# Gate matmuls of the recurrent branch: one F32 pass or three F32R passes over split operands

## The chip, the cores and the metric

The kernel runs on one core of one Trainium2 chip. The metric is the device time of one execution in microseconds (us); lower is better.

## What is computed

One layer of a block with three parts: a mixer, a merge of its branches, and a feed-forward part with a convolution. All arrays are float32. There are 1024 tokens and 256 context tokens, of width 1024. The change lies in the mixer, whose recurrent branch takes its input through a short convolution and then computes two gates for each of two directions:

```python
def rglru_coeffs(xc, wa, ba, wx, bx, lam):
    xb = xc.reshape(b_, t_, LRU_BLOCKS, LRU_BLOCK_W)           # 8 blocks of 128 channels
    r = sigmoid(einsum('btnk,nkj->btnj', xb, wa) + ba)
    i = sigmoid(einsum('btnk,nkj->btnj', xb, wx) + bx)
    log_a = -LRU_C * r * softplus(-lam)
    a = exp(log_a)
    b = sqrt(-expm1(2.0 * log_a)) * i * xc
    return a, b                                                # h[t] = a[t] * h[t-1] + b[t]
...
xr = dwconv(xr, lru_conv_w, lru_conv_b, LRU_CONV_LEFT)         # 4 taps
cr = dwconv(cr, lru_conv_w, lru_conv_b, LRU_CONV_LEFT)
h_x, h_c = rglru_bidirectional(xr, cr, ...)
y_rnn_x = h_x * gelu(gx)
```

Beside it the mixer computes a neighbourhood attention of 16 heads, with normalized and rotated queries and keys and a bias by relative position.

## The kernel before

**Turns.** The mixer runs eight turns, one for each block of 128 channels and, at the same time, for a pair of attention heads. Each engine has its own program `turn(i, first, last)`, and the order of the work on each engine is the order in which these programs issue it. Turn 0 and turn 7 have orders of their own; the six turns between them are the same.

**High and low parts.** Most matmuls take both operands in two parts: a high part, cast to F32R by ScalarE (`split_hi`), and a low part, the difference of the value and its high part, subtracted by VectorE (`split_low`, L1311). Three passes (high by high, low by high, high by low) go into the same bank: `three_passes` (L45 to L47) for the query tiles, `chunk` (L857 to L859) for the projections `fm`. The gates do not: `gate_pieces` (L890) issues one F32 matmul of the convolution's output `xc` with the weights `lw`. One such matmul stands in the trace as two records of TensorE.

**One middle turn, on TensorE.** The projection of the gelu gate (`fm` of `G`, two halves), with the last group of the previous turn's attention between them; ten query tiles `q_tile`, the first two with 256 columns and the others with 384; behind tiles 0, 1, 2 the gate pieces of direction 0, two at a time, and behind tiles 4, 5, 6 those of direction 1 (`GATES_AFTER`). There are six pieces a direction: pieces 0 to 2 give `r`, pieces 3 to 5 give `i`, over the context (256 columns) and two halves of the tokens (512 each, `SEGS`). A piece waits until the bank that it writes is free (`f_free`), which means until ScalarE has evacuated the piece two before it. Then come the projection of the next turn's recurrent input (`XR`), transposes, the first scores, the projections `MR` and `MN`, and the attention: for each of 16 units `prob_transposes` (L948, L953), `scores` (L930 to L935), and `weighted_values` (L968, L986).

**On the other engines in that turn.** ScalarE splits the query weights, evacuates `gel`, the tiles (`q_evac`, L1096 and L1101) and the gate pieces (L1091), then computes the decays (`decays`, L1114 to L1118) and the root (`root`, L1122), and splits the weights of `XR` and `MR` behind the fifth tile. VectorE subtracts the low parts of the query weights, runs the convolution (`conv`, L1341 and L1344), the sums of the last attention group of the turn before (`outputs`, L1500 and L1503), then `head_squares` for every tile, `gated_input` (L1359), `complement` (L1363), `scan` (L1370, L1374), `mean_squares` (L1392), the low parts of `XR` and `MR`, and from `inverse_roots` (L1400 to L1402) on the normalizations and rotations of keys and queries (L1407 to L1427), which the transposes wait for. GpSimd raises the mean squares to a power (`inverse_root`, L808), adds masks to the bias (L816, L819, L823) once the bias has landed and the convolution is done, finishes the sigmoids of the output gates (L798, L801), and copies low parts of keys (`exchange_low`, L790). SP issues the loads: the gate weights `lw` at the start of a turn, and the weights of each unit once `w_lo` says that its slot of `raw` has been split.

**Slots.** `fh` and `fl` hold the high and low parts of projection weights in two slots. Slot 0 holds `XR` and then `MN`. `ORDER` gives the place of each unit in the counts `w_hi` and `w_lo`; loads and matmuls wait for these counts through `split_count`.

## Time and profile before

| | us |
|---|---|
| median of 3 runs | 2171.84 |
| lowest and highest | 2170.0 and 2172.96 |
| the profiled execution | 2171.01 |
| span of its core | 2169.2 |
| granted TensorE clock over the span | 0.99 of full |
| TensorE (PE) busy | 2086.3, 96% |
| VectorE (DVE) busy | 1569.0, 72% |
| ScalarE (ACT) busy | 1053.6, 49% |
| GpSimd (POOL) busy | 346.0, 16% |

The span is the stretch of the profiled execution in which the engines work; the little that is left lies around it. The mixer covers the span up to about 1220 us, and one middle turn takes 140.5 us. Busy shares are means over stages with different limits: what a change inside a turn is worth is read from the queues of the engines in that turn, at the moments where one waits for another. In a timeline, times are counted from the start of the span.

### The profile page before, as it was taken

What the parts mean: (1) busy time and instruction counts of PE and PEld (TensorE: products, weight loads), DVE (VectorE), ACT (ScalarE), POOL (GpSimd) and SP (SyncE); (2) the same over time, 40 slices, a digit from 0 to 9 for tenths busy, and PEclk for the clock granted to TensorE, in tenths of its full rate; (3) what the DMA queues carried; (4) which work ended last, traced back from release to release, by engine and by line L of the source; (5) the groups of instructions that cost most, each with busy time, mean ns of one, the idle gap of its engine ahead of it and who ended that gap; (6) DMA issues with size and microseconds to landing.
All of it is one profiled execution on the core that took longest, in us unless ns stands there. A gap on an engine that the chain in (4) does not pass through costs nothing.

```text
span 2169.2 us, 28185 instructions
## 1 busy us (share of the span) xinstructions
PE 2086.3 (96%) x10750; PEld 1769.4 (82%) x10750; DVE 1569.0 (72%) x2758; ACT 1053.6 (49%) x1614; POOL 346.0 (16%) x234
## 2 busy tenths in 40 slices
PE   5999999999999999999997999998999999999999
PEld 1788888988889889888886788886888888888887
DVE  6688598685985968859759766667998888863433
ACT  3466665765766656766576410003444334433221
POOL 0031221221312221122122000000111111110000
PEclk9999999999999999999999999998999999999999
DMA  8421212012112120121202574452222221146552
GB/s 322 109 63 40 70 41 81 11 57 64 35 43 64 52 69 30 40 71 40 71 1 98 184 274 157 148 197 70 78 78 88 87 77 69 68 161 207 185 183 89
DMA packets 85654, 209.91 MB, mean 97 GB/s; under 512 B 24592, under 2 KB 30096, under 8 KB 85392
## 3 DMA queue, kind: packets, MB, share of 16 engines
q1 hardware_dynamic: 63360, 182.95, 24.8%
q0 software_dynamic: 5760, 20.97, 2.8%
q10 hardware_dynamic: 16400, 4.19, 0.9%
q8 instruction: 85, 1.39, 0.3%
q14 instruction: 49, 0.40, 0.1%
HBM read 171.39 MB, written 40.89 MB: 98 GB/s over the span
## 4 chain that ended last, share of the span: by engine, by line
PE 79%; DVE 11%; ACT 4%; issue 1%; DMA 0%; POOL 0%; SPq 0%; ACTq 0%; DVEq 0%; POOLq 0%
PE banks L47 14%; PE banks L45 14%; PE banks L46 14%; PE banks L986 4%; PE banks L2108 4%; PE banks L2106 4%; PE banks L2107 4%; PE banks L857 4%; PE banks L859 4%; PE banks L858 4%; PE banks L890 3%; DVE probT_low L1486 2%; PE banks L948 2%; DVE prob L1478 1%; PE banks L930 1%
## 5 line engine op out<-in xcount | busy, mean ns | idle before, releaser
L45 PE MATMUL banks<-qh,xnh 128*128 128x384 f32 (+1 forms) x640 | 223.1, 349 | 0.3 <-PEq L211 0.3
L857 PE MATMUL banks<-xnh,wh 128*128 128x512 f32 (+1 forms) x536 | 211.7, 395 | 4.0 <-ACT stage L1091 3.6
L47 PE MATMUL banks<-qh,xnl 128*128 128x384 f32 (+1 forms) x640 | 207.4, 324 | 0.0
L46 PE MATMUL banks<-ql,xnh 128*128 128x384 f32 (+1 forms) x640 | 207.3, 324 | 0.0
L859 PE MATMUL banks<-xnh,wl 128*128 128x512 f32 (+1 forms) x536 | 204.8, 382 | 0.0
L858 PE MATMUL banks<-xnl,wh 128*128 128x512 f32 (+1 forms) x536 | 204.4, 381 | 0.0
L1486 DVE TENSOR_TENSOR probT_low<-banks,probT_high 128x512 fp32r<-128x512 f32 (+2 forms) x256 | 138.8, 583 | 56.2 <-ACT probT_high L1159 55.1
L46 PE MATMUL banks<-yl,wh 128*128 128x512 f32 x404 | 157.3, 389 | 0.0
L47 PE MATMUL banks<-yh,wl 128*128 128x512 f32 x404 | 157.2, 389 | 0.0
L45 PE MATMUL banks<-yh,wh 128*128 128x512 f32 x404 | 157.2, 389 | 0.0
L1159 ACT CAST probT_high<-banks 128x512 fp32r<-128x512 f32 (+2 forms) x256 | 117.1, 510 | 59.9 <-PE banks L948 51.0
L1354 DVE TENSOR_REDUCE ssq<-sqs 128x4 f32<-128x256 f32 (+1 forms) x80 | 31.0, 389 | 143.5 <-ACT sqs L1101 143.2
L2021 POOL TENSOR_TENSOR conv_d<-conv_d 128x1024 f32<-128x1024 f32 x22 | 69.7, 3169 | 382.9 <-ACT conv_d L2147 307.3
L1149 ACT ACTIVATE prob<-prob,stat 128x768 f32<-128x768 f32 (+1 forms) x128 | 128.2, 1002 | 1.4 <-DVE stat L1481 1.2
L45 PEld LDWEIGHTS banks<-qh,xnh 128*128 128x128 f32 x640 | 120.7, 189 | 9.0 <-issue 8.1
L46 PEld LDWEIGHTS banks<-ql,xnh 128*128 128x128 f32 x640 | 120.7, 189 | 8.3 <-issue 7.7
L47 PEld LDWEIGHTS banks<-qh,xnl 128*128 128x128 f32 x640 | 120.6, 188 | 0.0
L859 PEld LDWEIGHTS banks<-xnh,wl 128*128 128x128 f32 x536 | 101.5, 189 | 19.9
L857 PEld LDWEIGHTS banks<-xnh,wh 128*128 128x128 f32 x536 | 102.0, 190 | 18.2 <-issue 3.8
L2401 DVE TENSOR_TENSOR yl<-sw_d,yh 128x512 fp32r<-128x512 f32 x44 | 30.4, 691 | 118.6 <-ACT yh L2223 118.6
L1736 ACT CAST wh<-raw 128x1024 fp32r<-128x1024 f32 x22 | 23.2, 1055 | 189.1 <-PE banks L47 159.3
L986 PE MATMUL banks<-probT_high,vS 128*128 128x256 f32 x448 | 114.0, 293 | 0.0
(346 smaller groups left out, 5764.6 us busy)
## 6 DMA issues: line engine op xcount, KB each, us to landing
raw<-w_ff SPq DMA_DIRECT2D x33, 512.0 KB, 3.7
raw<-w_down SPq DMA_DIRECT2D x33, 512.0 KB, 4.5
raw<-w_fm SPq DMA_DIRECT2D x32, 512.0 KB, 6.5
raw<-w_qkv SPq DMA_DIRECT2D x24, 512.0 KB, 3.9
raw<-w_mix SPq DMA_DIRECT2D x24, 512.0 KB, 4.9
h_d<-conv_d SPq DMA_DIRECT2D x22, 512.0 KB, 2.6
sw_d<-h_d SPq DMA_DIRECT2D x44, 256.0 KB, 3.1
raw<-w_modT SPq DMA_DIRECT2D x16, 512.0 KB, 4.5
```

Source lines behind the costliest of these rows:

```text
L45: pe.matmul(out, w_hi(k), x_hi(k), start=(k == 0), stop=False)
L46: pe.matmul(out, w_hi(k), x_lo(k), start=False, stop=False)
L47: last = pe.matmul(out, w_lo(k), x_hi(k), start=False, stop=(k == chunks - 1))
L857: pe.matmul(out, fh[:, s, k, :], xnh[:, k, c0:c1], start=(k == 0), stop=False)
L858: pe.matmul(out, fh[:, s, k, :], xnl[:, k, c0:c1], start=False, stop=False)
L859: return pe.matmul(out, fl[:, s, k, :], xnh[:, k, c0:c1], start=False, stop=(k == KC - 1))
L986: last = pe.matmul(dst, vS[:, s, h, :], moving, start=(n == 0 and part == 0), stop=(n == len(blocks) - 1 and part == 1))
L1149: act.activation(p, p, ACT.Exp, bias=stat[:, u, 1:2], scale=-1.0, accum_out=stat[:, u, 2:3]).then_inc(exp_done, 1)
L1159: act.copy(probT_blocks(pth, u, bank), probT_bank(u, bank)).then_inc(pt_hi, 1)
L1486: dve.tensor_tensor(probT_blocks(ptl, u, bank), probT_bank(u, bank), probT_blocks(pth, u, bank).bitcast(F32), ALU.subtract).then_inc(pt_lo, 1)
L2106: pe.matmul(out, w_hi_c[:, m, :], h_slot(xh, c), start=(k == 0), stop=False)
L2107: pe.matmul(out, w_hi_c[:, m, :], h_slot(xl, c), start=False, stop=False)
```

## The change

Each gate matmul becomes three F32R passes, high weights by high input, high weights by low input, low weights by high input. For that the gate weights and the convolution's output are split in every turn: ScalarE casts the weights (`gate_weights_high`) and the three segments of `xc` (`gate_input_high`), VectorE subtracts the four low parts (`gate_weights_low`, `gate_input_low`) right behind the convolution, the last of them behind the sums of the previous turn's last attention group. The parts lie in slot 0 of `fh` and `fl` and in memory that `stage` and `pad` and their neighbours use at other times. `XR` needs slot 0 too, so its split moves behind the gates: on ScalarE behind the last gate pieces' evacuation, on VectorE behind the first rotation, and `MR` is split before it. In the middle turns `gated_input` of direction 0 goes ahead of the fourth `head_squares`. The convolution signals its context part and its token part apart, and what waited for the whole waits for the second signal. On TensorE the waits for the landed weights and for the convolution are gone; the first three pieces wait for the low parts instead.

```diff
+        lwh, lwl = fl[:, 0, 0:4, :], fl[:, 0, 4:8, :]
+        xcl_tokens = fh[:, 0, :, :].rearrange("p k c -> p (k c)")
...
-        ORDER = {Q0: 0, Q1: 1, Q2: 2, XR: 3, MR: 4, MN: 5, G: 6}
+        ORDER = {Q0: 0, Q1: 1, Q2: 2, MR: 3, XR: 4, MN: 5, G: 6}
...
-                pool.wait_ge(conv_done, i + 1)
+                pool.wait_ge(conv_done, 2 * i + 2)
...
-                if d == 0 and pieces[0] == 0:
-                    pe.wait_ge(lw_in, i * 16 + 16)
-                    pe.wait_ge(conv_done, i + 1)
                 for n in pieces:
                     c0, c1 = SEGS[n % 3]
                     j = gate_use(i, d, n)
                     pe.wait_ge(f_free, f_count(i, j) - 2)
-                    pe.matmul(f_bank(j)[:, 0:c1 - c0], lw[:, 2 * (n // 3) + d, :], xc[:, c0:c1],
-                              start=True, stop=True).then_inc(f_full, 1)
+                    if d == 0 and n < 3:
+                        pe.wait_ge(gate_lo, 4 * i + n + 2)
+                    m = 2 * (n // 3) + d
+                    out = f_bank(j)[:, 0:c1 - c0]
+                    pe.matmul(out, lwh[:, m, :], xch_of(n % 3), start=True, stop=False)
+                    pe.matmul(out, lwh[:, m, :], xcl_of(n % 3), start=False, stop=False)
+                    pe.matmul(out, lwl[:, m, :], xch_of(n % 3), start=False, stop=True).then_inc(f_full, 1)
...
+            def gate_weights_high(i):
+                act.wait_ge(lw_in, i * 16 + 16)
+                act.copy(lwh, lw[:, :, :]).then_inc(gate_hi, 1)
+
+            def gate_input_high(i, seg):
+                c0, c1 = SEGS[seg]
+                act.wait_ge(conv_done, 2 * i + (1 if seg == 0 else 2))
+                act.copy(xch_of(seg), xc[:, c0:c1]).then_inc(gate_hi, 1)
...
                 gelu(i, 0)
+                gate_weights_high(i)
+                gate_input_high(i, 0)
                 if not last:
                     gelu(i, 1)
+                gate_input_high(i, 1)
+                gate_input_high(i, 2)
...
-                if not last:
-                    split_hi(XR, raw_count(XR, i))
                 split_hi(MR, raw_count(MR, i))
                 q_evac(i, 6)
                 gate_pieces(i, *(GATES_FIRST if first else GATES_AFTER)[6])
                 if first:
                     q_evac(i, 7)
                     gate_pieces(i, *GATES_FIRST[7])
+                if not last:
+                    split_hi(XR, raw_count(XR, i))
...
+            def gate_weights_low(i):
+                dve.wait_ge(gate_hi, 4 * i + 1)
+                dve.tensor_tensor(lwl, lw[:, :, :], lwh.bitcast(F32), ALU.subtract).then_inc(gate_lo, 1)
+
+            def gate_input_low(i, seg, first):
+                c0, c1 = SEGS[seg]
+                dve.wait_ge(conv_done, 2 * i + 2)
+                dve.wait_ge(gate_hi, 4 * i + seg + 2)
+                if seg == 0 and not first:
+                    dve.wait_ge(stage_out, i * 64)
+                dve.tensor_tensor(xcl_of(seg), xc[:, c0:c1], xch_of(seg).bitcast(F32), ALU.subtract).then_inc(gate_lo, 1)
...
                 conv(i, first)
+                gate_weights_low(i)
+                gate_input_low(i, 0, first)
+                gate_input_low(i, 1, first)
                 if not first:
                     outputs(i - 1, GROUPS_ATT - 1, False)
-                for s in range(4):
+                gate_input_low(i, 2, first)
+                early = not first and not last
+                for s in range(3):
                     head_squares(i, s)
+                if early:
+                    gated_input(i, 0)
+                head_squares(i, 3)
...
-                if not last:
-                    split_low(XR, i)
                 split_low(MR, i, last)
...
                 rotate(1, 0, krot[0])
+                if not last:
+                    split_low(XR, i)
```

## Rows read from the trace of the kernel before

**Rows 1.** The page, busy time, share of the span and instructions.
```profile
PE 2086.3 (96%) x10750; PEld 1769.4 (82%) x10750; DVE 1569.0 (72%) x2758; ACT 1053.6 (49%) x1614; POOL 346.0 (16%) x234
```
**Rows 2.** Timeline, TensorE, middle turn: start us, duration us, instruction, [idle before <- releaser].
```profile
376.14 0.28 PE L45 MATMUL banks<-qh,xnh 128*128 128x256 f32 x1
...
379.02 1.45 PE L890 MATMUL banks<-xc,lw 128*128 128x256 f32 x4
...
383.17 1.45 PE L890 MATMUL banks<-xc,lw 128*128 128x512 f32 x4
...
388.62 1.88 PE L890 MATMUL banks<-xc,lw 128*128 128x512 f32 x4
...
398.67 1.45 PE L890 MATMUL banks<-xc,lw 128*128 128x256 f32 x4
...
404.12 1.50 PE L890 MATMUL banks<-xc,lw 128*128 128x512 f32 x4
...
455.59 0.63 PE L948 MATMUL banks<-cst,prob 128*128 128x128 f32 x4 [1.27 <-DVE probT_low L1486]
```
**Rows 3.** Timeline, VectorE, the same turn.
```profile
411.46 0.18 DVE L1400 TENSOR_TENSOR rstd<-rstd 128x24 f32<-128x24 f32 x1 [0.41 <-POOL rstd L808]
...
418.07 0.42 DVE L1354 TENSOR_REDUCE ssq<-sqs 128x4 f32<-128x256 f32 x1 [0.22 <-ACT sqs L1101]
...
445.62 0.16 DVE L1481 TENSOR_TENSOR stat<-stat 128x1 f32<-128x1 f32 x1
...
446.21 0.15 DVE L1563 TENSOR_SCALAR stat<-one 128x1 f32<-128x1 f32 x1 [0.43 <-PE banks L935]
```
**Rows 4.** Timeline, ScalarE, the same turn.
```profile
376.35 0.60 ACT L1091 ACTIVATE gel<-banks 128x512 f32<-128x512 f32 x1 [3.18 <-PE banks L859]
...
403.53 1.05 ACT L1091 ACTIVATE gR<-banks,lp 128x256 f32<-128x256 f32 x2
...
446.07 0.93 ACT L1149 ACTIVATE prob<-prob,stat 128x768 f32<-128x768 f32 x1
```
**Rows 5.** Timeline, VectorE and GpSimd, before this turn and in turn 0.
```profile
365.49 1.23 DVE L1311 TENSOR_TENSOR ql<-raw,qh 128x1024 fp32r<-128x1024 f32 x1
...
366.63 2.06 DVE L1311 TENSOR_TENSOR ql<-raw,qh 128x1024 fp32r<-128x1024 f32 x1
...
365.71 1.90 POOL L801 TENSOR_TENSOR stage<-stage,half_one 128x512 f32<-128x512 f32 x1
...
123.05 1.76 DVE L1311 TENSOR_TENSOR wl<-raw,wh 128x1024 fp32r<-128x1024 f32 x1
...
121.94 1.79 POOL L816 TENSOR_TENSOR bias<-bias,cst 128x256 f32<-128x256 f32 x1 [1.06 <-DMA bias<-bias_d]
...
123.69 3.07 POOL L819 TENSOR_TENSOR bias<-bias,cst 128x896 f32<-128x896 f32 x1
```
**Rows 6.** Timeline, VectorE and GpSimd, behind the convolution.
```profile
376.71 0.43 DVE L1500 TENSOR_TENSOR bot<-banks,bot 64x256 f32<-64x256 f32 x1
...
376.83 0.74 POOL L816 TENSOR_TENSOR bias<-bias,cst 128x256 f32<-128x256 f32 x1 [9.22 <-DVE xc L1344]
...
377.52 2.12 POOL L819 TENSOR_TENSOR bias<-bias,cst 128x896 f32<-128x896 f32 x1
...
379.71 4.03 POOL L823 TENSOR_TENSOR bias<-bias,cst 128x1792 f32<-128x1792 f32 x1
```
**Rows 7.** Timeline, VectorE and GpSimd, at the mean squares' power.
```profile
407.26 4.16 POOL L808 TENSOR_TENSOR rstd<-rstd,power 128x24 f32<-128x24 f32 x1 [23.52 <-DVE rstd L1392]
...
407.31 1.26 DVE L1311 TENSOR_TENSOR wl<-raw,wh 128x1024 fp32r<-128x1024 f32 x1 [0.19 <-ACT wh L1085]
```
**Rows 8.** Timeline, TensorE, in turn 0 and in the last turn.
```profile
95.67 1.56 PE L890 MATMUL banks<-xc,lw 128*128 128x256 f32 x4 [0.16 <-DMA lw<-lru_w]
...
142.27 1.12 PE L910 MATMUL banks<-cst,qkv 128*128 128x128 f32 x4 [3.49 <-DVE qrotA L1427]
...
1079.27 1.10 PE L890 MATMUL banks<-xc,lw 128*128 128x256 f32 x3 [0.21 <-issue]
```

More of the change, by code:

```diff
@@ L508, in mixer_programs @@
         ptl = sbuf(st, "probT_low", [P, RING * 7, P], F32R)
+        with ExitStack() as gate_parts:
+            xcl_context = sbuf(gate_parts, "xcl_context", [P, C], F32R)
         stage = sbuf(st, "stage", [P, HALF])
@@ L522, in mixer_programs @@
         yT = sbuf(st, "yT", [P, 2, 256])
+        with ExitStack() as gate_parts:
+            xch = sbuf(gate_parts, "xch", [P, 1288], F32R)
         pad = sbuf(st, "pad", [P, 1288])
@@ L528, in mixer_programs @@
         sinT = cst[:, P + 3 * GW + NT * HD:].rearrange("p (t f) -> p t f", f=HD)
+        lwh, lwl = fl[:, 0, 0:4, :], fl[:, 0, 4:8, :]
+        xcl_tokens = fh[:, 0, :, :].rearrange("p k c -> p (k c)")
+        xch_of = lambda seg: xch[:, (2, 5, 5)[seg] + SEGS[seg][0]:(2, 5, 5)[seg] + SEGS[seg][1]]
+        xcl_of = lambda seg: xcl_context[:, :] if seg == 0 else xcl_tokens[:, SEGS[seg][0] - C:SEGS[seg][1] - C]
         S, lower, F_ps = banks
@@ L541, in mixer_programs @@
         lw_in = sem("b_lw_in")
+        gate_hi, gate_lo = sem("b_gate_hi"), sem("b_gate_lo")
         decayed = sem("b_decayed")
@@ L1198, in turn @@
                         split_hi(u, raw_count(u, i))
+                if not first:
                     bottoms(i - 1, GROUPS_ATT - 1)
@@ L1244, in turn @@
                     gate_pieces(i, *GATES_FIRST[7])
+                if not last:
+                    split_hi(XR, raw_count(XR, i))
+                if first:
                     decays(i, 1)
@@ L1348, in conv @@
                             then(last)
-                last.then_inc(conv_done, 1)
+                    last.then_inc(conv_done, 1)
+            def gate_weights_low(i):
[8 more added lines that the diff above has]
+                dve.tensor_tensor(xcl_of(seg), xc[:, c0:c1], xch_of(seg).bitcast(F32), ALU.subtract).then_inc(gate_lo, 1)
             def head_squares(i, s):
@@ L1520, in turn @@
                     head_squares(i, 4)
-                gated_input(i, 0)
+                if not early:
+                    gated_input(i, 0)
                 complement(i, 0)
```

## The prediction, made before the changed kernel ran

> **What bounds the kernel now.** I read the page first, then the queue of TensorE in one middle turn of the mixer, then the queues of VectorE, GpSimd and ScalarE at the same moments. TensorE is busy for 96% of the span [rows 1], so any step it gets shorter by could count. The mixer runs eight turns. The six middle ones repeat with a period of 140.5 us, so I follow the one whose first query tile starts at 376.14 and multiply by six. In it TensorE goes from tile to gate to tile without a gap, and stops once for long: at 455.59 it has stood 1.27 us for VectorE's low half of the first transposed probabilities [rows 2]. So the turn has two limits in series: TensorE up to about the last query tile, and from there VectorE, which between 411.46 and that wait idles only 0.22 and 0.43 us in the rows shown, for ScalarE and for scores [rows 3]. A gain on TensorE before that wait only makes the wait longer, unless VectorE's own chain starts earlier too.
>
> **The gate matmuls.** Tile 0 takes 379.02 - 376.14 = 2.88 us for 24 passes of 256 columns, 0.12 each. From 379.02 to 383.17 lie two gate pieces (256 and 512 columns) and tile 1, so the pieces take 4.15 - 2.88 = 1.27 us. From 383.17 to 388.62 the same pair and tile 2 of 24 passes of 384 columns: 5.45 - 1.28 = 4.17 us, 0.174 a pass. From 388.62 to 398.67 two 512-column pieces and two tiles: 10.05 - 8.34 = 1.71 us [rows 2]. A pass therefore costs some 0.45 ns a column, and F32 gates 1.67 ns a column. Three F32R passes cost 0.36 us for 256 columns and 0.68 for 512: the pair falls from 1.28 to 1.04, the double 512 from 1.71 to 1.36. A turn has four pairs and two doubles, 4 x 0.24 + 2 x 0.35 = 1.65 us, over eight turns 13 us at most. That the three passes might not be cheaper is excluded by these rows.
>
> One piece of it is not paid out. At 404.12 TensorE reaches the third piece of direction 1, which needs the bank that ScalarE empties from 403.53 on, some 0.45 us of work [rows 4]. That chain hangs on tile 4, not on the gates, so what the pair at 398.67 saves is lost again in a wait.
>
> **The new splits.** ScalarE gets four casts (weights, three input pieces). A 512-column evacuation takes 0.60 us and stands at 376.35 [rows 4]; with two more behind it the last cast is done by about 378.0, ahead of tile 0's evacuation at 379.2. ScalarE idles there, so I charge nothing. If the cover were gone, tile 0's evacuation would be late by the 1.8 us of the casts, and tile 3 is the first to want it.
>
> VectorE gets four subtractions right behind the convolution, which ends at 376.7. One of 1024 columns takes 1.23 us, 1.14 from start to start (365.49 to 366.63) [rows 5]; I estimate 0.65 for 512 and 0.4 for 256. Alone they would be done for piece 1 at 378.5, before TensorE asks at 379.4. But they do not stand alone. The same convolution count releases GpSimd's three bias additions: 0.74 us at 376.83, 2.12 at 377.52, 4.03 at 379.71 [rows 6]. In the kernel before, what VectorE does beside them is a sum with one operand in PSUM, 0.43 us, untouched [rows 6]. The new subtractions have both operands in SBUF, and such instructions and GpSimd's exclude each other in this trace. The weight split at 366.63 takes 2.06 us instead of 1.23 while GpSimd's multiplication from 365.71 takes 1.90. In turn 0 the split at 123.05 takes 1.76 beside a bias addition of 1.79 instead of 0.74; and the next addition, 3.07 instead of 2.12, has waited for that split [rows 5]. They also take turns: where both wait, the one that did not run last goes next. The split at 123.05 ended at 124.81, so it went between two additions that GpSimd issues back to back.
>
> With that the order after the convolution is: weights low to 377.4; addition 1 to 378.1; context low to 378.5; addition 2 (2.1) to 380.6; first token half low to 381.2; then the old sums of the last attention group, free of the conflict, to 382.1, while addition 3 (4.0) runs to 385.2; second token half low to 385.9. TensorE asks for the first half at 379.4 and gets it at 381.3, ends the pair at 382.0 and tile 1 at 384.9; asks for the second half and gets it at 386.0; ends the pair at 387.0, tile 2 at 391.2, the double at 392.6, where it was at 390.3. It enters tile 3 about **2.2 us late** instead of 0.24 + 0.24 + 0.35 = 0.8 early. The removed waits for the weights' load and the convolution cost nothing in this turn. Behind the waiting gates on TensorE stand the query tiles, and behind those everything else. The last group's sums come 4.5 us later; tile 2 and the store of that group wait for them and have over 2 us left. The context part also waits for the last store of the stage; GpSimd wrote it by 367.6 [rows 5], which leaves the store over 9 us.
>
> The shared port is the subject of the Trainium skill, SBUF — State Buffer, section "Who interferes with whom": a VectorE instruction with two SBUF inputs contends with a GpSimd instruction that reads SBUF, and the loser blocks for the whole instruction. The additions agree with that, 2.06 for 1.23. The power of the mean squares does not: it runs 4.16 us from 407.26, and a split of two SBUF inputs takes 1.26 beside it at 407.31 [rows 7]. By the Trainium skill both splits would have stood until 411.4 and taking one away from there would shorten the chain by 1.1 us a turn, 7 us in all; by the row it shortens nothing, since the power, not the splits, is what ends last there. I go by the row.
>
> **The rnn weights moved.** VectorE's split of them, 1.14 us, leaves a place where VectorE then waits 0.41 for the power anyway (411.46), and goes behind the rotation, into a stretch without idle time but the 0.22 at 418.07 [rows 3]. The load of G that SP holds for this split comes later by about 12 us and is first read in the attention, over 40 us on. ScalarE's cast (about 1 us) delays the decays and tile 7's evacuation, not past tile 8's. TensorE needs the split after tile 9 and has it some 4 us earlier. Cost on VectorE's chain: 1.14 - 0.22, about 0.9. The earlier multiplication of the gated input removes nothing from the path, because ScalarE's root waits for tile 4. POOL's bound on the bias count is the same moment as before.
>
> **One middle turn.** VectorE's chain starts from the root behind tile 4, so 2.2 late; plus 0.9 makes 3.1; the 0.43 us of idle time at 446.21 gives back up to that, 2.7; but the exponential at 446.07 [rows 4], which ScalarE began 0.3 us behind its input of 445.62 + 0.16 [rows 3], then comes 2.8 late, and with it the transposed queries behind it. TensorE, by then only 1.4 late, waits for it. I take 2.75, times six: **16.5**.
>
> **First and last turn.** In turn 0 the gates wait for the weights' load until 95.67 [rows 8]. ScalarE now waits for it with the first cast, and a cast, a half's cast and a subtraction follow before the second piece can start: about 98.3 where it was 96.1, 2.1 us late. The additions come only at 121.9 there. The wait of 3.49 us at 142.27 [rows 8] shows VectorE as the limit, and its chain gets 1.14 for the moved split and up to 0.8 from a changed order with the additions: between 1.0 and 2.1, I take 1.9. In the last turn TensorE reaches the gates at 1079.27, right when the convolution ends [rows 8], so the whole queue shows: the second piece starts at about 1083.8 where it was 1079.8, 4.0 late, of which some 1.0 comes back through shorter pieces: 3.0.
>
> **The sum.** 16.5 + 1.9 + 3.0 = 21.4. The profiled execution took 2171.01 us around a span of 2169.2, and would take 2192.4; it is 0.8 below the median of 2171.84, so the forecast is **2193**.
>
> **Rivals.** (1) *VectorE wins every time, or the new subtractions do not conflict*: the gates are met as computed without GpSimd. It decides at 379.4: the first half must be split by then. TensorE enters tile 3 0.8 early, VectorE's chain gains 0.8, loses 0.9, gains up to 0.4: 0 to 0.3 a turn, -1; turn 0 +1.5, last +1: 2173, no change. For it speaks only that VectorE issues first; the 2.06 at 366.63 speaks against. Chance 0.14. (2) *The full TensorE gain arrives*, 1.45 a turn, 2160. It needs slack on VectorE that [rows 3] do not show: 0.04. (3) *GpSimd keeps the port between additions 1 and 2*, or the later sigmoids of GpSimd collide with the late VectorE. The first moves the second piece to 385.3, 2.9 more a turn, 2211; the second costs one instruction of about 1.0 a turn, 2200. The row at 123.05 speaks against the first. Together 0.12. (4) *Only the long third addition is met*, the others slip past: about 1 us a turn, 2178 to 2186, 0.06.
>
> **How the numbers follow.** The forecast's own range, 2187 to 2199, has 0.64. Unknown sizes (0.65 and 0.4 for the subtractions, the releases of about 0.1) move it by some 0.5 a turn. The range 2175 to 2205 takes in (4), part of (1) and most of (3) and leaves out about 0.2. A difference of 0.2%, 4.3 us, is about what a measurement of this kernel can tell from none. Faster has (2) and an edge of (1): 0.05; same the rest of (1): 0.12; slower 0.83.
>
> **What would show it.** Right: the subtractions of the token halves at 2 to 4 us instead of 0.65 beside GpSimd's additions; TensorE idle about 1.9 and 1.1 us before the second and third gate piece; a middle turn of 143.2 us; the idle time before 455.59 grown to about 2.6. Wrong: subtractions of 0.65 beside 4.0 us additions (rival 1), or a turn under 140.5.

## The result and the profile after

The changed kernel takes 2207.24 us (median of 5 runs, 2204.89 to 2212.96) against 2171.84: a ratio of 1.0171, 95% interval 1.016 to 1.0183. It is 35.4 us slower, where the forecast was 21 and the range ended at 2205. The profiled execution took 2207.24 us around a span of 2205.4. The first section of its page (engine, busy time and share of the span, instructions) stands against [rows 1]:

```profile
PE 2084.5 (95%) x10846; PEld 1785.6 (81%) x10846; DVE 1627.7 (74%) x2790; ACT 1066.3 (48%) x1646; POOL 353.1 (16%) x234
```

TensorE is busy for 1.8 us less, VectorE for 58.7 us more, and the span is 36.2 us longer. The convolution's first instruction on VectorE cuts the mixer into turns. The start moved by -1.3 us (over all profiles of the study it lies between 86.2 and 88.3 us), turn 0 grew by 4.6, five middle turns by 4.0 each and one by 8.5, and what lies behind the last convolution's start by 4.2.

A middle turn splits at five instructions of VectorE's queue, which every kernel of this study has. In the kernel before, for the turn at 370.02, they are the convolution (L1341), the mean squares (L1392), their roots (L1400), the first small operation behind the scores (L1481) and the second pair of `qpS` subtractions (L1445). The table gives the time from each to the next, as the difference of two starts in the timeline of VectorE. It is the same within 0.1 us in all middle turns but at most one, of which below; f13 has a second one, 0.2 us longer. The runs of the next section stand in it too.

| kernel | conv. to mean square | to roots | to small op. | to `qpS` | to next conv. | turn |
|---|---|---|---|---|---|---|
| before | 36.92 | 4.52 | 34.16 | 5.04 | 59.86 | 140.50 |
| **changed** | 38.65 | 5.56 | 34.97 | 5.52 | 59.86 | 144.55 |
| e1, additions later | 36.21 | 5.56 | 34.97 | 5.52 | 59.87 | 142.13 |
| e2, MR split behind squares | 38.63 | 4.92 | 34.96 | 4.80 | 59.87 | 143.20 |
| e3, orders alone | 36.92 | 4.52 | 35.02 | 5.52 | 59.86 | 141.84 |
| e4, cut F32 gates | 36.11 | 5.56 | 33.83 | 5.09 | 59.85 | 140.44 |
| f11, the same, eight copies | 36.13 | 4.52 | 33.84 | 4.80 | 59.87 | 139.15 |
| f13, changed, eight copies | 38.65 | 4.52 | 34.98 | 5.06 | 59.87 | 143.10 |
| f6, e1 and early MR split | 36.22 | 4.52 | 34.98 | 5.07 | 59.87 | 140.66 |
| f9, three repairs, `lw` first | 36.21 | 4.52 | 34.98 | 4.80 | 59.88 | 140.39 |
| f12, XR split early too | 36.24 | 4.52 | 33.85 | 4.82 | 59.87 | 139.29 |

The changed kernel loses 1.73 + 1.04 + 0.81 + 0.48 = 4.06 us a turn, in four places.

**Behind the convolution** (timeline of VectorE, GpSimd and TensorE in one middle turn; start, us, engine, line, operation, operands; in brackets the idle time before and what ended it):

```profile
383.92 0.68 DVE L1380 TENSOR_TENSOR wl<-lw,wl 128x512 fp32r<-128x512 f32 x1
384.52 0.97 DVE L1388 TENSOR_TENSOR xcl_context<-xc,xch 128x256 fp32r<-128x256 f32 x1
385.41 2.59 DVE L1388 TENSOR_TENSOR wh<-xc,xch 128x512 fp32r<-128x512 f32 x1
...
388.95 3.52 DVE L1388 TENSOR_TENSOR wh<-xc,xch 128x512 fp32r<-128x512 f32 x1
...
384.15 1.05 POOL L826 TENSOR_TENSOR bias<-bias,cst 128x256 f32<-128x256 f32 x1 [9.21 <-DVE xc L1371]
385.16 2.29 POOL L829 TENSOR_TENSOR bias<-bias,cst 128x896 f32<-128x896 f32 x1
387.54 4.38 POOL L833 TENSOR_TENSOR bias<-bias,cst 128x1792 f32<-128x1792 f32 x1
...
388.15 0.47 PE L901 MATMUL banks<-xch,wl 128*128 128x512 f32 x1 [1.29 <-DVE wh L1388]
...
392.62 0.47 PE L901 MATMUL banks<-xch,wl 128*128 128x512 f32 x1 [0.67 <-DVE wh L1388]
```

This is the forecast's sequence. The four subtractions and the three additions of [rows 6] alternate. The token halves take 2.59 and 3.52 us for work of 0.68, and TensorE stands 1.29 and 0.67 us before the pieces that want them.

**At the power** (ScalarE's cast of MR, VectorE's mean square, split and roots, GpSimd's power):

```profile
415.08 1.08 ACT L1097 CAST wh<-raw 128x1024 fp32r<-128x1024 f32 x1
...
415.99 0.18 DVE L1431 TENSOR_SCALAR rstd<-ssq 128x24 f32<-128x24 f32 x1
416.26 1.23 DVE L1338 TENSOR_TENSOR wl<-raw,wh 128x1024 fp32r<-128x1024 f32 x1
...
421.55 0.18 DVE L1439 TENSOR_TENSOR rstd<-rstd 128x24 f32<-128x24 f32 x1 [1.69 <-POOL rstd L818]
...
416.31 5.21 POOL L818 TENSOR_TENSOR rstd<-rstd,power 128x24 f32<-128x24 f32 x1 [24.39 <-DVE rstd L1431]
```

In [rows 7] the power started at 407.26 and the split at 407.31, having waited 0.19 us for ScalarE's cast. Here the split starts at 416.26, 0.05 us ahead of the power, and the power takes 5.21 us instead of 4.16. The cast now starts 0.91 us ahead of the mean square, where the kernel before had 0.77, and the split no longer waits for it; e3 and e4 below show what moved it.

**At the scores** (VectorE's small operation, ScalarE's exponential behind it, GpSimd's first sigmoid):

```profile
456.51 0.88 DVE L1520 TENSOR_TENSOR stat<-stat 128x1 f32<-128x1 f32 x1
...
457.42 0.94 ACT L1170 ACTIVATE prob<-prob,stat 128x768 f32<-128x768 f32 x1 [2.71 <-DVE stat L1520]
...
454.85 1.40 POOL L808 TENSOR_TENSOR stage<-stage,one 128x512 f32<-128x512 f32 x1 [9.18 <-ACT stage L1103]
456.32 1.04 POOL L811 TENSOR_TENSOR stage<-stage,half_one 128x512 f32<-128x512 f32 x1
```

and GpSimd's first sigmoid instruction in the kernel before:

```profile
446.31 1.04 POOL L798 TENSOR_TENSOR stage<-stage,one 128x512 f32<-128x512 f32 x1 [11.55 <-ACT stage L1091]
```

There it came 0.69 us behind the small operation, which [rows 3] have at 445.62. The small operation of one column, 0.16 us in [rows 3], takes 0.88: it starts 0.19 us behind a sigmoid instruction and ends with it. 0.24 of the 0.72 us is slack of the exponential, which had waited for ScalarE; 0.48 stays.

**In one turn the weights land late** (ScalarE's cast of `lw`, VectorE's subtractions, TensorE's waits, fifth middle turn):

```profile
817.60 0.62 ACT L1123 CAST wl<-lw 128x512 fp32r<-128x512 f32 x1 [3.47 <-DMA lw<-lru_w]
...
819.00 2.32 DVE L1388 TENSOR_TENSOR xcl_context<-xc,xch 128x256 fp32r<-128x256 f32 x1
821.24 4.45 DVE L1388 TENSOR_TENSOR wh<-xc,xch 128x512 fp32r<-128x512 f32 x1
...
825.84 0.77 PE L901 MATMUL banks<-xch,wl 128*128 128x512 f32 x1 [3.78 <-DVE wh L1388]
```

ScalarE waits for the load 3.47 us instead of the usual 2.2 to 2.5. So little is enough for the two short additions to get the port first, and the first token half then costs 4.45 us instead of 2.59. TensorE stands 1.33 and 3.78 us before its first two gate pieces, 3.15 us more than in the other middle turns; with the clock, of which next, the turn is 4.45 us longer. The same turn is the long one in every profile of the three passes in which the additions start with the convolution's end (148.7 in e2, 150.1 in f1, 148.2 in f13). Why the load is late there was not tried.

**The granted clock falls behind the long waits** (windows of the changed kernel: stretch, its length, busy time of TensorE, its weight loads, VectorE, ScalarE and GpSimd, granted clock, DMA share, GB/s):

```profile
98.20:101.60 3.40, 3.40 (x12) 3.33 (x12) 0.56 (x2) 2.75 (x5) 0.00 (x0) 0.50 1.20 261
825.30:828.70 3.40, 2.86 (x10) 2.60 (x11) 2.13 (x5) 0.69 (x1) 0.00 (x0) 0.50 0.11 39
1115.40:1118.80 3.40, 3.40 (x10) 3.12 (x11) 3.33 (x3) 0.87 (x2) 3.40 (x1) 0.50 0.11 39
```

0.50 of full is the 1.2 GHz level. The three stretches lie in turn 0, in the long turn and in the last turn, each behind TensorE's waits for low parts: 2.24 and 0.46 us, 1.33 and 3.78, 1.72 and 1.91. In the middle turns that wait 1.29 and 0.67 us the clock stays at 1.00, and so it does there in all turns of the kernel before and of e1, where the longest such waits are 1.44 us together in turn 0 and 1.18 in the last. In turn 0, tile 1 takes 5.71 us from its first matmul to the next gate piece, against 4.18 in e1: 1.5 us. What the waits leave unexplained in the long turn and, against e1, in the last one is 1.3 us each. In the long turn of e2, with waits of 1.34 and 3.78 us, the clock is at 0.50 for 6.8 us, and the turn is 5.5 us longer instead of 4.45.

### The profile page after: what moved, and what is told of

It is laid out like the page before. It is cut to its first block, busy times and chain, and to the rows that moved or that the text cites. A ratio compares the mean times of both kernels' runs of the same rounds, so it can differ in the third digit from the quotient of the medians.

```text
span 2205.4 us, 28481 instructions
## 1 busy us (share of the span) xinstructions
PE 2084.5 (95%) x10846; PEld 1785.6 (81%) x10846; DVE 1627.7 (74%) x2790; ACT 1066.3 (48%) x1646; POOL 353.1 (16%) x234
## 4 chain that ended last, share of the span: by engine, by line
PE 60%; DVE 26%; ACT 5%; issue 3%; POOL 2%; DMA 1%; SPq 0%; DVEq 0%; ACTq 0%; POOLq 0%
PE banks L45 12%; PE banks L47 12%; PE banks L46 12%; PE banks L998 4%; PE banks L2154 4%; PE banks L2156 4%; PE banks L2155 4%; DVE probT_low L1525 2%; DVE wh L1388 2%; DVE prob L1517 2%; PE banks L960 1%; POOL rstd L818 1%; DVE xc L1371 1%; DVE wl L1338 1%; DVE swp L1464 1%
## 5 line engine op out<-in xcount | busy, mean ns | idle before, releaser
L45 PE MATMUL banks<-qh,xnh 128*128 128x384 f32 (+1 forms) x640 | 209.4, 327 | 0.3 <-PEq L211 0.3
L818 POOL TENSOR_TENSOR rstd<-rstd,power 128x24 f32<-128x24 f32 (+1 forms) x16 | 65.1, 4071 | 337.1 <-DVE rstd L1431 337.1
```

The source lines that it names most:

```text
L45: pe.matmul(out, w_hi(k), x_hi(k), start=(k == 0), stop=False)
```

## The experiments

Each is given with its median of 4 to 11 runs and the ratio to the kernel before, which had 2170.5 to 2171.0 us on the same chips.

**e1: the bias additions behind the low parts.** It tests the cause of the first place.

```diff
-                pool.wait_ge(conv_done, 2 * i + 2)
+                pool.wait_ge(gate_lo, 4 * i + 4)
```

> The changed kernel with one wait moved: GpSimd's three bias additions start only when all four low parts of the gate operands are stored, instead of with the end of the convolution. Theory (the two engines' two-input operations exclude each other, and each subtraction behind the convolution but the first waits for one bias addition): the token-half subtractions take 0.68 us instead of 2.59 and 3.52, TensorE's waits of 1.29 and 0.67 us before the second and third gate piece go, the one turn of 149.0 us, in which the weights landed late and the three additions got ahead, becomes like the others; a middle turn goes from 144.5 to about 142, the last turn loses some 3 us, the whole is about 20 us faster (near 2187). The power comes later on GpSimd by some 2 us, which costs nothing, since its own mean square is later than that. Rival (ScalarE's casts and the subtractions are late by themselves: the low parts are produced too late whatever GpSimd does): waits and time stay, 2205 to 2209.

Measured: 2184.81 us, 1.0065 (1.0052 to 1.0078), 22.4 below the changed kernel. In the turn at 373.75:

```profile
380.93 0.42 DVE L1388 TENSOR_TENSOR xcl_context<-xc,xch 128x256 fp32r<-128x256 f32 x1
381.56 0.69 DVE L1388 TENSOR_TENSOR wh<-xc,xch 128x512 fp32r<-128x512 f32 x1 [0.22 <-ACT xch L1128]
...
383.20 0.69 DVE L1388 TENSOR_TENSOR wh<-xc,xch 128x512 fp32r<-128x512 f32 x1
...
384.04 0.74 POOL L826 TENSOR_TENSOR bias<-bias,cst 128x256 f32<-128x256 f32 x1 [12.70 <-DVE wh L1388]
...
386.94 4.06 POOL L833 TENSOR_TENSOR bias<-bias,cst 128x1792 f32<-128x1792 f32 x1
```

The subtractions take 0.42 and 0.69 us, both waits of TensorE before gate pieces are gone, the long turn takes 142.45 us, and the rest behind the last convolution's start is 0.3 us longer than before instead of 4.2. The theory holds: the subtractions were late because they and the additions exclude each other. Some 4 of the 22.4 us are the clock, which no longer falls behind the waits (an estimate, the sum of the three costs above). The convolution to the mean square is now 0.71 us *shorter* than in the kernel before: the passes' gain arrives here. Over the whole turn it can be read in TensorE's queue, from the first gate piece to the projection behind the last tile: 43.6 us against 44.8 in the kernel before, so the passes save 1.2 us a turn.

**e2: the MR split behind the power.**

```diff
-                split_low(MR, i, last)
+                if first or last:
+                    split_low(MR, i, last)
                 head_squares(i, 6)
+                if not first and not last:
+                    split_low(MR, i, last)
```

> The changed kernel with the low split of the MR weights put behind the squares of the sixth head pair on VectorE, in the middle turns alone, so that GpSimd's power starts before it. Theory (a power that starts under a running split waits for its end: 5.21 us against 4.16 before the change): the power takes 4.16 again, VectorE's wait for it ends 1.05 us earlier, the whole is about 6 us faster (six turns), unless the small two-input operation behind the scores, which GpSimd's sigmoid blocks for 0.72 us, meets it otherwise. Rival (the power's 5.21 is something else, and the chain behind it is set by TensorE): no change, within 2 us.

Measured: 2200.44 us, 1.0135 (1.0121 to 1.0149), 6.8 below the changed kernel, as expected, but half for another reason. The power takes 4.17 us. The split now ends 0.5 us behind it and holds the roots back, so 0.64 of the 1.04 us comes back there. The other 0.72 comes back at the scores, which VectorE now reaches when the sigmoid does not hold the small operation (4.80).

**e3: the orders alone**, with the F32 gates of before: `ORDER`, the XR split behind the rotation on both engines, `gated_input` ahead of the fourth `head_squares`.

> The kernel before, with its F32 gate matmuls, and only the orders of the change: XR split behind MR, its low part moved behind the second key rotation, the first gated input before the fourth head squares. Theory: the power starts under the running MR split (+1.05 us a middle turn), the XR split now lies on VectorE's chain (+0.9), the softmax has 0.3 of slack: +1.6 a middle turn, with turn 0 and the last some 10 us slower in all (2180 to 2186). If the collision of the small operation behind the scores with the sigmoid appears here too, +0.7 a turn more. Rival (the orders are free, the split was only moved): no change.

Measured: 2181.52 us, 1.0043 (1.0029 to 1.0057), 10.6 us slower. The total was right and half of its reason wrong: the power did not grow. 34.16 became 35.02 for the XR split, and 5.04 became 5.52 for the small operation (0.88 us again). The MR split still waited for ScalarE's cast and started 0.05 us behind the power:

```profile
410.79 1.04 ACT L1085 CAST wh<-raw 128x1024 fp32r<-128x1024 f32 x1
...
411.57 0.18 DVE L1393 TENSOR_SCALAR rstd<-ssq 128x24 f32<-128x24 f32 x1
411.94 1.26 DVE L1312 TENSOR_TENSOR wl<-raw,wh 128x1024 fp32r<-128x1024 f32 x1 [0.19 <-ACT wh L1085]
...
411.89 4.17 POOL L808 TENSOR_TENSOR rstd<-rstd,power 128x24 f32<-128x24 f32 x1 [23.52 <-DVE rstd L1393]
```

**e4: TensorE's gain without splits.** The F32 gate matmuls of before, cut to 216 of 256 and 410 of 512 columns (the last 40 and 102 columns of each gate segment are left out), which saves about what three passes save: 1.4 us a turn in TensorE's queue, against 1.2 in e1.

```diff
-                    pe.matmul(f_bank(j)[:, 0:c1 - c0], lw[:, 2 * (n // 3) + d, :], xc[:, c0:c1],
+                    m = 216 if n % 3 == 0 else 410
+                    pe.matmul(f_bank(j)[:, 0:m], lw[:, 2 * (n // 3) + d, :], xc[:, c0:c0 + m],
```

> The kernel before, its F32 gate matmuls cut to 216 of 256 and 410 of 512 columns, so that TensorE saves about what three F32R passes save (0.24 us a pair, 0.35 a double piece), without splits or casts. The last 40 and 102 columns of each gate segment are left out. Theory (from the head squares on, VectorE's chain sets the turn, and the gate pieces' saving of 1.65 us a turn ends in its idle time of 0.43): 0.3 to 0.8 us a turn, 2167 to 2171. Rival (TensorE's gain arrives whole at the end of the turn): 2158 to 2162.

Measured: 2169.18 us, 0.9991 (0.9983 to 1.0000). The time is that of the theory, its reason is not. The mean square comes 0.81 us earlier and the stretch behind the roots is 0.33 shorter, since VectorE no longer waits for the squares of [rows 3]. Then 1.04 is given back at the power and the small operation takes 0.43 us. The splits start earlier than the power, by 0.04 us:

```profile
406.72 2.03 ACT L1086 CAST wh<-raw 128x1024 fp32r<-128x1024 f32 x2
...
407.63 0.18 DVE L1393 TENSOR_SCALAR rstd<-ssq 128x24 f32<-128x24 f32 x1
407.91 2.39 DVE L1312 TENSOR_TENSOR wl<-raw,wh 128x1024 fp32r<-128x1024 f32 x2
...
407.95 5.21 POOL L808 TENSOR_TENSOR rstd<-rstd,power 128x24 f32<-128x24 f32 x1 [22.71 <-DVE rstd L1393]
```

The same cast and mean square in the kernel before:

```profile
406.17 1.99 ACT L1085 CAST wh<-raw 128x1024 fp32r<-128x1024 f32 x2
...
406.94 0.18 DVE L1392 TENSOR_SCALAR rstd<-ssq 128x24 f32<-128x24 f32 x1
```

e3 and e4 together show what reversed the order of the two starts. The cast starts 0.77 us ahead of the mean square in the kernel before, 0.78 in e3, and 0.91 in e4 and in the changed kernel. e3 exchanges XR and MR and keeps the split's wait; e4 leaves them in their old order and loses it. So it is not the exchange, it is the shorter gate pieces: the cast stands behind their evacuation on ScalarE.

**f1, f5, f8, f11, f13: copies ahead of the splits.** Does the order of two starts decide it, or what stands beside the power? One, four or eight copies of one column on VectorE between the mean square and the splits delay nothing but the splits. f1 (one copy) and f13 (eight) have them in the changed kernel, f5 (one), f8 (four) and f11 (eight) in the kernel of e4, whose gate segments lack their last columns, ahead of both splits.

```diff
+                for c in range(8):
+                    dve.tensor_scalar(stat[:, c, 3:4], one[:, :], 1.0, None, ALU.mult)
                 split_low(MR, i, last)
```

> The changed kernel with one instruction more on VectorE: a copy of one column (128x1, 0.14 us) between the mean square and the low split of the MR weights, in every turn. Theory (it decides alone who is first: with it GpSimd's power starts some 0.1 us ahead of the split instead of 0.05 us behind it, and takes 4.16 us instead of 5.21): a middle turn loses 1.04 us, to about 143.5, or 143.1 where the small operation behind the scores meets the sigmoid less; the whole is 6 to 9 us faster for one instruction more, 2198 to 2201. Rival (the power's length is not decided by the order of the two starts): no change, 2206 to 2208.

> The kernel before with its F32 gate matmuls cut to 216 and 410 columns as before (the last 40 and 102 columns of each gate segment are left out), and with the same one-column copy on VectorE ahead of the two weight splits. Theory (the cut matmuls' gain of 0.82 us up to the mean square was given back there, since the earlier mean square met splits that no longer waited for ScalarE, and the power took 5.21): with the copy the power takes 4.16 again, a middle turn is about 139.4 instead of 140.44, the whole 6 to 7 us faster than without the copy, 2161 to 2164. Rival (TensorE's gain is lost elsewhere): equal to the run without the copy, 2168 to 2170.

Measured: f1 2209.09 us, 1.0176 (1.0162 to 1.0190); f5 2169.45 us, 0.9995 (0.9986 to 1.0003). Neither moved, but neither tells: the copy went into a gap that was there anyway, the split still starts 0.28 us behind the mean square, and the power 0.32 to 0.33.

> The kernel before with the cut F32 gate matmuls (the last 40 and 102 columns of each gate segment are left out) and four one-column copies on VectorE ahead of the weight splits instead of one, since one left the split's start where it was (0.28 us behind the mean square's, the power's is 0.32). Four should put it 0.4 to 0.6 us behind. Theory (who starts first decides): the power takes 4.16 us, mean square to root 4.5 instead of 5.56, a middle turn 139.4 to 139.7 instead of 140.44, the whole 4 to 6 us below 2169. Rival (the power is stretched by whatever stands beside it, in either order): no change, 2168 to 2171.

Measured: 2170.09 us, 0.9997 (0.9988 to 1.0006). The split now starts 0.01 us *behind* the power, and the power still takes 5.25 us, and once 6.39, when it stood behind both splits. The recorded start is not yet the moment from which a split no longer holds the power up.

> The kernel before with the cut F32 gate matmuls (the last 40 and 102 columns of each gate segment are left out) and eight one-column copies on VectorE ahead of the weight splits. Four put the splits' start 0.34 us behind the mean square's, 0.01 us behind the power's, and the power took 5.25 and once 6.39 us. In the kernel before, with 0.05 us between them, it took 4.16. Eight copies should put them some 0.25 us behind the power. Theory (the power takes the port a little after its recorded start and then isn't disturbed by what starts later): power 4.16 to 4.2 us, mean square to root 4.5 us, a middle turn about 139.4 us instead of 140.45, the whole 2162 to 2165. Rival (in the kernel before it was ScalarE's cast, not the order of the starts, that spared the power): power 5.2 again, no change, 2168 to 2171.

Measured: 2160.96 us, 0.9955 (0.9941 to 0.9968). Eight more instructions in every turn make the kernel 8.2 us faster than e4 without them. The splits and the power in f8 (timeline of VectorE, two splits in one line, and of GpSimd):

```profile
407.54 2.38 DVE L1312 TENSOR_TENSOR wl<-raw,wh 128x1024 fp32r<-128x1024 f32 x2
...
407.53 5.25 POOL L808 TENSOR_TENSOR rstd<-rstd,power 128x24 f32<-128x24 f32 x1 [22.71 <-DVE rstd L1393]
```

and in f11:

```profile
405.13 2.35 DVE L1312 TENSOR_TENSOR wl<-raw,wh 128x1024 fp32r<-128x1024 f32 x2
...
404.88 4.17 POOL L808 TENSOR_TENSOR rstd<-rstd,power 128x24 f32<-128x24 f32 x1 [22.71 <-DVE rstd L1393]
```

> The changed kernel with eight one-column copies on VectorE between the mean square and the low split of the MR weights. Theory (the split now starts some 0.25 us behind the power and no longer holds it up): power 4.17 us instead of 5.21, mean square to root 4.52 us, a middle turn 143.1 to 143.5 us instead of 144.55, the whole 6 to 9 us faster, 2198 to 2201. Rival (the order matters only in the kernel before): no change, 2205 to 2209.

Measured: 2200.02 us, 1.0143 (1.0128 to 1.0159), 7.2 below the changed kernel; mean square to roots 4.52 us. So the second place is settled in the changed kernel itself. A split that starts 0.25 us behind the power leaves it at 4.17 us, with as much VectorE work beside it as before.

**f6 and f7: two repairs more.** f6 is e1 with MR split early in the middle turns, in the time that VectorE waits for ScalarE's root (its cast behind the fourth tile). f7 is f6 with the first sigmoid held back.

```diff
                     head_squares(i, 4)
+                if early:
+                    split_low(MR, i, last)
                 scan(i, 0)
...
+                    pool.wait_ge(bound_done, i * ATT + 2)
                     sigmoid(i, F_MR, 0, 4)
```

> The changed kernel with the bias additions behind the low parts (as in the first of these runs), and in the middle turns the MR weights split early, in VectorE's idle time before ScalarE's root (its cast behind the fourth tile on ScalarE), so that no split stands beside the power. Theory: conv start to mean square 36.2 us, power and its wait 4.5, the XR split still on the chain (35.0 to the scores), 4.8 to 5.5 around the softmax, 59.9 behind: 140.4 to 141.1 a middle turn; the whole 6 to 10 us below the run with the additions alone, 2175 to 2179. Rival (the idle time is none: the split delays the root's product): 0 to 1.2 us a turn come back, 2180 to 2188.

> The same, and in all turns but the last GpSimd's first sigmoid waits until the minima of the second scores are stored, so that it meets neither of the small operations behind the scores. Theory: the small operation takes 0.16 us in every middle turn, 140.4 us a middle turn, and in turn 0, where that sigmoid stretched a rotation product from 0.89 to 2.57 us, some 1.5 us go: 2173 to 2176, level with the kernel before or 1 us above it. Rival (a later sigmoid delays TensorE's banks or the stores and costs as much): equal to the run without it or above.

Measured: f6 2175.61 us, 1.0026 (1.0015 to 1.0037); f7 2171.16 us, 1.0007 (0.9998 to 1.0016). Both as expected. In f6 the small operation takes 0.42 us, in f7 0.16; the middle turns of f7 take 140.4 us. The operation in f6:

```profile
452.57 0.42 DVE L1522 TENSOR_TENSOR stat<-stat 128x1 f32<-128x1 f32 x1
```

and in f7, with the sigmoid that now waits for the next one:

```profile
448.92 0.16 DVE L1523 TENSOR_TENSOR stat<-stat 128x1 f32<-128x1 f32 x1
...
450.37 2.22 POOL L808 TENSOR_TENSOR stage<-stage,one 128x512 f32<-128x512 f32 x1 [12.29 <-DVE stat L1523]
```

In the two profiles turn 0 differs by 2.2 us, more than the middle turns' 0.27 explain together. There a sigmoid of the changed kernel had stretched a rotation product from 0.89 to 2.57 us (timeline of VectorE, changed kernel):

```profile
163.67 2.57 DVE L1464 TENSOR_TENSOR swp<-qkv,cst 128x128 f32<-128x128 f32 x4
```

**f9 and f10: the gate weights first.** In turn 0 `lw` is loaded behind 672 KB of constants. f9 is f7 with the two exchanged, f10 the kernel before with the same.

```diff
+            load_gate_weights(0)
             sp.dma_start(cst[:, :], consts).then_inc(const_in, 16)
```

> The changed kernel with the three repairs (bias additions behind the low parts, MR split early, first sigmoid behind the second scores' minima) and, in turn 0, the gate weights loaded ahead of the constants (672 KB) instead of behind them. Theory (TensorE's wait of 3.6 us for the low parts in turn 0 is the late load, which now goes through ScalarE and VectorE before it reaches TensorE): turn 0 loses some 3 us, to about 143 us; the whole is 2167 to 2169, below both kernels. Rival (the constants, now later, are needed as early): no change or slower, 2171 to 2174.

> The kernel before with the same exchange of the two loads in turn 0 alone. TensorE waits there for the gate weights for 0.16 us in the profile shown. Theory: 0 to 2 us faster, 2169 to 2171, less spread between runs. It is the control for the run above: what of that run's gain belongs to the load and not to the repaired gate passes.

Measured: f9 2168.56 us, 0.9993 (0.9984 to 1.0002); f10 2170.19 us, 0.9996 (0.9987 to 1.0005). The exchange gives the repaired kernel 2.6 us and the kernel before 0.9, which is within its interval. With all that the change is level with the kernel before, no more: the 1.14 us of the XR split (33.84 to 34.98) eat the passes' gain.

**f12: the gate parts elsewhere.** XR could not be split before the last gate because the parts lie in its slot. f12 is f9 with them in memory that is idle in the middle turns, and splits XR there before the fourth tile's squares; the gate weights are then cast and subtracted in two halves, and ScalarE casts XR behind the second tile.

```diff
+        qkv_tail = qkv_r[:, 7:10, :].rearrange("p t c -> p (t c)")[:, 0:1024]
...
+            return (qkv_tail if moved(i) else xcl_tokens)[:, SEGS[seg][0] - C:SEGS[seg][1] - C]
...
+            return (qkv_r[:, 0:2, 0:P], lwh_tail[:, :, :]) if moved(i) else (lwh[:, 0:2, :], lwh[:, 2:4, :])
...
+            return lw_r[:, :, :] if moved(i) else lwl
...
                 if early:
                     gated_input(i, 0)
+                    split_low(XR, i)
```

> The repaired kernel (bias additions behind the low parts, MR split early, first sigmoid behind the second scores, gate weights first in turn 0), and in the middle turns the gate parts in memory that is idle then (the tail of the query and key tiles, the gate weights' own place, the upper half of the sigmoid's stage), so that the XR split needn't wait for the gate passes and stands in VectorE's idle time between the third and the fourth tile. Theory (the XR split's 1.15 us on the chain is all that is left): 36.2 + 4.5 + 33.8 + 4.8 + 59.9 = 139.2 us a middle turn instead of 140.4, the whole 7 us below 2168.6, 2161 to 2163. Rival (the early splits, the copy in two halves and the earlier loads meet other work): 2165 to 2170.

Measured: **2161.48 us**, 0.9958 (0.9946 to 0.9971) against the kernel before and 45.8 us below the changed one, 139.3 us a middle turn. It beats both. The XR split in VectorE's idle time, and the wait for the power's end with no split beside it:

```profile
387.99 1.22 DVE L1373 TENSOR_TENSOR wl<-raw,wh 128x1024 fp32r<-128x1024 f32 x1
...
402.17 0.18 DVE L1474 TENSOR_SCALAR rstd<-ssq 128x24 f32<-128x24 f32 x1
...
406.69 0.18 DVE L1482 TENSOR_TENSOR rstd<-rstd 128x24 f32<-128x24 f32 x1 [0.67 <-POOL rstd L842]
...
402.49 4.17 POOL L842 TENSOR_TENSOR rstd<-rstd,power 128x24 f32<-128x24 f32 x1 [19.23 <-DVE rstd L1474]
```

## Why the prediction was right and wrong

Its direction and its main mechanism held, its size did not: 14 us too little.

- *The gate passes* (0.24 a pair, 0.35 a double, 1.65 a turn, 0.24 of it lost in a wait): right in kind, a little too high. In e1 the pairs save 0.24, 0.20, 0.06 and 0.17 and the doubles 0.27 each, 1.2 us where I had 1.4; the 0.06 is the pair that I had written off. e4, which saves 1.4, moves the mean square by 0.81, and f11 shows 1.35 at the end of the turn.
- *TensorE enters tile 3 2.2 us late*: the sequence held to the instruction; the mean square came 1.73 late. The subtractions took 0.68 and 0.42 us for my 0.65 and 0.4. e1 shows the cause.
- *The XR split moved*, 0.9: 0.81 here, 0.86 in e3.
- *The power*, of which I wrote that taking a split away "shortens nothing": right for an absent split (4.17 us in f6), and the step that failed all the same. From [rows 7] I read that the power doesn't mind a split. The row shows that it doesn't mind one that starts 0.05 us after it. I did not ask what had let the power go first: the split's 0.19 us wait for ScalarE's cast. The shorter gate pieces take that wait away (e4), since the cast follows their evacuation and starts 0.13 us earlier against the mean square; I had followed their gain on TensorE alone. Missing: 1.04 a turn, 6 us in all. The Trainium skill, SBUF — State Buffer, "Who interferes with whom", has the loser block for the whole instruction. By that rule a power that starts second waits for the split, and here it does, 1.05 and once 2.23 us. By the same rule a split that starts second would wait for the power, and here it does not, 1.26 us in [rows 7]. My verdict "by the row" set the rule aside for both orders when the row spoke of one.
- *The exponential's slack of 0.3*: 0.24. But the operation ahead of it was late itself, by 0.72. I had priced such a meeting with the sigmoids at 1.0 a turn and left it to a rival of 0.12 shared chance, although VectorE would come 3 us later into a stretch where GpSimd is active. [rows 3] gave the operation's time, 445.62, and the same trace has the sigmoid at 446.31. It is a second failed step: 0.48 a turn net, 3 us.
- *The removed waits cost nothing; ScalarE's casts are free*: true in five turns of six. The wait for the load had not gone, it had moved to ScalarE, ahead of the additions' race for the port: 4.45 us in one turn, of which 3.15 are waits and the rest goes with the clock at 0.50.
- *First and last turn*, 1.9 and 3.0: they grew by 4.6 and 4.2. I had put nothing for the clock, and it took 1.5 and 1.3 us. In the last turn that is the 1.2 that was missing, and e1, with a wait of 1.18 us instead of 3.63 and the clock at 1.00, gives back 3.9. In turn 0 the first gate piece came 2.1 us later, as forecast; the sigmoids' 1.68 was missing beside the clock. f7 gets 2.2 us back there against f6, and f9 5.5 against f7, in their profiles. The load varies between profiles: ScalarE waits for it 7.7 us in f7, 6.3 in the changed kernel and 5.1 in e1, and in f7 the clock falls behind it as well.
- *The sum*: 6 x 2.75 = 16.5 stands against 28.7 for the middle turns. Over six turns the power was short by 6.2 us, the end of the chain by 5.0 (0.35 a turn was to come back, 0.48 was lost), the late load and the clock behind it by 4.5; the first place and the XR split were 3.3 too high.
- *Rival 2*, the full gain of 1.45 a turn, I gave 0.04 because [rows 3] show no slack on VectorE. That was the wrong test. Those rows begin with the roots; what lies before them, tiles, squares and root, is set by TensorE, and gets earlier with it. f11 and f12 show 1.35 and 1.2 us of it.

## What to carry to other kernels

When two engines share a port, read from the trace who starts first and by how much, and what holds the other back: a margin of 0.05 us decided 1.05 us a turn here, and 0.13 us gained in a third engine's queue reversed it. New two-input work on VectorE belongs where GpSimd is quiet, or GpSimd's long work is made to wait for it: one moved wait returned 22 of 35 us. And before a gain is written off against a later limit, see what sets that limit's start; a gain of 1.4 us a turn looked lost in e4 (0.06) and was there (1.35) as soon as a collision behind it was removed.

## What the runs showed of the hardware

- The power of 24 columns runs 4.16 us and lets two-input splits run beside it at full speed, but waits for one that is under way. Being 0.01 us ahead in the records is not enough (5.25 us), 0.05 is (4.16).
- An operation of one column, 0.16 us, takes 0.88 us beside a GpSimd instruction of 512 columns in every middle turn of the changed kernel, and 1.00 in the last turn of f6. Each time it ends with that instruction.
- Behind the convolution the granted clock fell to 0.50 (1.2 GHz) for 3.4 us after TensorE had stood for 2.24 and 0.46, 1.33 and 3.78, and 1.72 and 1.91 us, and stayed at 1.00 after 1.29 and 0.67. It cost 1.3 to 1.5 us each time.
- A one-column copy behind a small VectorE instruction costs nothing when a dependent one follows: the split's start moved by less than 0.02 us. Four moved it by 0.06, eight by 0.3.
